# Keys, values and the second half's x turned by VectorE in 32 by 32 blocks and by the transfers

## The chip, the cores and the metric

The kernel runs on one core of a Trainium2 chip. The metric is the device time of one execution in microseconds (us). The engines are named as in the profile: PE (TensorE, with PEld for its weight loads), DVE (VectorE), ACT (ScalarE), POOL (GpSimd) and SP (SyncE, which here only issues transfers).

## The reference, cut to what matters

One decoder layer over a prompt of 2048 tokens of width 1024 (and 32 sample tokens), all in fp32. One wide projection feeds two mixers:

```python
h = rmsnorm(x, g_norm)
proj = jnp.einsum('bld,de->ble', h, w_in)                 # 1024 -> 10240 columns
u_p, z_p, q, k, v, z_r, gates = jnp.split(proj, IN_SPLITS, axis=-1)
...
qh, kh = rope(q, pos), rope(k, pos) * RET_QK_DIM ** -0.5  # 4 heads of 256
scores = jnp.einsum('bhid,bhjd->bhij', q, k) * decay      # inside a chunk
inner  = jnp.einsum('bhij,bhjv->bhiv', scores, v)         # v: 4 heads of 512
s_new  = gamma ** C * s + jnp.einsum('bhjd,bhjv->bhdv', k_dec, v)
...
x_out = x + jnp.einsum('bld,de->ble', merged, w_out)      # then rmsnorm
```

The projection comes out with features on the partitions and tokens along the rows. The state update (`s_new`) contracts over tokens, so it wants keys and values with tokens on the partitions: they have to be turned. So has x, whose rows arrive with tokens on the partitions while the projection contracts over features.

## The kernel before

**Numbers.** Each fp32 matrix is split into a high and a low fp32r part; one product is three multiplications (high by high, low by high, high by low), lines 1310 to 1312.

**First part: the projection.** The prompt is two halves of 1024 tokens, each half 40 jobs (`NJ`): 32 for the heads and 8 for the gates. A job is 256 columns of `w_in` against the 1024 tokens by a seven-product scheme (Strassen's, Winograd's form): seven products of 12 multiplications of 128x512, in the order A11B11, A12B21, S2T2, S1T1, S3T3, S4B22, A22T4. Below, product i of a job is numbered 0 to 6 in this order. A head's eight jobs are q, v, k, v, zp, u, z, z. In the first half the heads come first and then the eight gates; in the second half seven gates, the heads, the last gate.

**Who does what in a job j.** SP loads the weights of job j+2 (1 MB, `weights`), then stores the results of job j-1 (`store`). ACT splits off the high part of the weights, DVE the low part, both six products ahead of PE (`SLOTS`). POOL makes the sums of weights. ACT copies partial sums out of PSUM after products 0, 2 and 3 (`part_s`, `part_v`, `part_s` again) and DVE adds after products 1, 4 and 5 into `c_out`. PE may start product 5 (S4B22) of a job only when the second `part_s` copy is made (`s5_copied`), and ACT makes that copy only when DVE has made its addition of product 1 (`c11_done`). That addition writes `c_out[j % 2]`, and so waits until the stores of job j-2 from the same buffer have landed (`c_free`).

**Turning keys and values.** After job j-1 was a k or v, PE turns its result in four steps after products 1 to 4 of job j (`turn`, four transposes of 128x128 each, L1360); ACT takes the high part from PSUM (`turn_high`), DVE the low part (`turn_low`, L2329) into one of three buffers `turned`, and SP stores 512 KB from it (L767). Keys also go through `rope` on DVE, and their unturned form is stored too, high and low (L774, L775), after `rope_low`.

**The second half's x.** From product 3 of job 32 on, every 11 products (`APART`) one of four pairs of token tiles is worked: SP loads it (`x_rows`), ACT squares (offset 1), DVE and POOL normalise (2 and 3) and make the sums (4), PE transposes the seven operands (offsets 5 to 9, L1305), ACT copies each out of PSUM and issues its store to `x_d` (L1810, L1813). SP may load the next pair when PE has transposed the last. After the fourth pair SP loads the seven operands back (`x_load`, L740) and ACT and DVE split them just before the second half starts.

**Second part: retention, branches, output.** Four token blocks of 512, four heads each. SP loads each head's q, k, turned k, v and z and, behind them in the same queue, the weights of the branches in pieces (`raw`, four buffers); ACT and DVE split them five pieces ahead of PE.

## Time and profile before

| | |
|---|---|
| median of 3 runs (lowest to highest) | 2841.2 us (2833.3 to 3100.54) |
| the profiled execution, its own time | 2833.4 us |
| its span | 2831.6 us |
| PE busy, of the span | 98% |
| DVE, ACT, POOL busy | 64%, 40%, 24% |
| TensorE clock granted | 0.997 |
| DMA queue q1 (SP): packets, MB, share of 16 engines | 266279, 541.73, 53.5% |
| DMA queue q10 (ACT): the same | 15168, 8.46, 1.0% |

Time outside the span is 1.8 us. Busy times of PE count the overlap of one multiplication with the next, so what PE's work costs is read from the distance of the starts in the timeline.

### The profile page before, as it was taken

The page shows a single profiled execution, that of the slowest core. Times are in us where ns is not written, and L with a number is a line of the kernel's source. Part 1 is how long each engine was busy: PE and PEld are TensorE (multiplying, and loading weights), DVE is VectorE, ACT ScalarE, POOL GpSimd, SP SyncE. Part 2 cuts the span into 40 slices and gives each one's busy share as a digit, 9 for nine tenths or more (in the row PEclk, how much of TensorE's full clock was granted, in tenths as well). Part 3 has the DMA queues.
Part 4 walks back from the last instruction along what each step waited for, and adds up shares of the span by engine and source line. Part 5 has one row for each costly group of instructions (what it writes and reads, how often), then busy time and mean ns, then how long its engine had stood idle before and what let it go on. Part 6 is the DMA issues. An engine that isn't in the chain of part 4 may idle for free.

```text
span 2831.6 us, 36714 instructions
## 1 busy us (share of the span) xinstructions
PE 2782.2 (98%) x13504; PEld 2249.1 (79%) x13504; DVE 1808.3 (64%) x2588; ACT 1126.4 (40%) x1901; POOL 684.8 (24%) x456
## 2 busy tenths in 40 slices
PE   6999999999999999999999999999999999999998
PEld 5888888888877777777777787877887888788876
DVE  8667566667555365655755566676677667766775
ACT  5444444444554444443434433333333333333332
POOL 5253433434332223425334330000000000000000
PEclk9999999999999999999999999999999999999999
DMA  4544444454564344453444458487648764876496
GB/s 144 197 146 155 173 147 158 156 179 145 180 223 153 113 156 162 147 186 125 163 154 154 165 200 307 141 278 289 246 145 283 289 239 150 283 290 234 153 340 261
DMA packets 281849, 552.80 MB, mean 195 GB/s; under 512 B 24216, under 2 KB 166872, under 8 KB 270527
## 3 DMA queue, kind: packets, MB, share of 16 engines
q1 hardware_dynamic: 266279, 541.73, 53.5%
q10 hardware_dynamic: 15168, 8.46, 1.0%
q8 instruction: 110, 1.80, 0.3%
q14 instruction: 68, 0.56, 0.1%
q0 software_dynamic: 224, 0.26, 0.0%
HBM read 375.59 MB, written 175.14 MB: 194 GB/s over the span
## 4 chain that ended last, share of the span: by engine, by line
PE 90%; DVE 4%; DMA 2%; issue 2%; ACT 1%; POOL 0%; ACTq 0%; SPq 0%; DVEq 0%; POOLq 0%
PE bank L1310 28%; PE bank L1312 28%; PE bank L1311 28%; PE bank L1360 2%; PE bank L1383 1%; PE bank L1502 1%; DMA raw<-in_w_branch_ret 1%; DVE w_lo L2173 1%; DVE xa_lo L2173 1%; DVE xs L2187 1%; PE bank L1632 1%; PE bank L1620 0%; PE bank L1610 0%; DMA x_d<-x_out 0%; DMA raw<-in_w_branch_pool 0%
## 5 line engine op out<-in xcount | busy, mean ns | idle before, releaser
L1310 PE MATMUL bank<-xa_hi,wa_hi 128*128 128x512 f32 x2240 | 888.8, 397 | 5.5 <-ACT part_s L1864 3.2
L1312 PE MATMUL bank<-xa_hi,wa_lo 128*128 128x512 f32 x2240 | 873.6, 390 | 0.0
L1311 PE MATMUL bank<-xa_lo,wa_hi 128*128 128x512 f32 x2240 | 873.5, 390 | 0.0
L1310 PEld LDWEIGHTS bank<-xa_hi,wa_hi 128*128 128x128 f32 x2240 | 420.6, 188 | 107.8 <-issue 21.5
L1312 PEld LDWEIGHTS bank<-xa_hi,wa_lo 128*128 128x128 f32 x2240 | 420.5, 188 | 90.0
L1311 PEld LDWEIGHTS bank<-xa_lo,wa_hi 128*128 128x128 f32 x2240 | 421.1, 188 | 82.8
L2173 DVE TENSOR_TENSOR wa_lo<-w_raw,wa_hi 128x512 fp32r<-128x512 f32 x320 | 312.7, 978 | 165.9 <-ACT wa_hi L1857 165.1
L2173 DVE TENSOR_TENSOR wa_lo<-w_sum,wa_hi 128x512 fp32r<-128x512 f32 x240 | 194.2, 809 | 241.3 <-ACT wa_hi L1857 241.3
L2173 DVE TENSOR_TENSOR w_lo<-raw,w_hi 128x512 fp32r<-128x512 f32 (+1 forms) x288 | 181.9, 659 | 189.3 <-ACT w_hi L1971 189.2
L1857 ACT ACTIVATE wa_hi<-w_raw 128x512 fp32r<-128x512 f32 x320 | 201.2, 629 | 242.6 <-PE bank L1312 238.3
L1971 ACT ACTIVATE w_hi<-raw 128x512 fp32r<-128x512 f32 (+1 forms) x288 | 166.4, 603 | 306.6 <-PE bank L1312 208.5
L1210 POOL TENSOR_TENSOR w_sum<-w_raw,w_sum 128x512 f32<-128x512 f32 x80 | 127.5, 1594 | 405.1 <-DVE wa_lo L2173 403.2
L1310 PE MATMUL bank<-og_hi,w_hi 128*128 128x512 f32 x512 | 201.4, 393 | 2.0 <-DVE z_in L2456 1.8
L1312 PE MATMUL bank<-og_hi,w_lo 128*128 128x512 f32 x512 | 200.0, 391 | 0.0
L1311 PE MATMUL bank<-z_lo,w_hi 128*128 128x512 f32 x512 | 199.8, 390 | 0.0
L1857 ACT ACTIVATE wa_hi<-w_sum 128x512 fp32r<-128x512 f32 x240 | 150.5, 628 | 105.5 <-PE bank L1312 93.4
L1218 POOL TENSOR_TENSOR w_sum<-w_raw,w_sum 128x512 f32<-128x512 f32 x80 | 113.1, 1414 | 307.8 <-DVE wa_lo L2173 307.8
L1265 POOL TENSOR_TENSOR inv_std<-var_eps,half 128x2 f32<-128x2 f32 x32 | 25.7, 803 | 640.6 <-DVE var_eps L2442 640.6
L1224 POOL TENSOR_TENSOR c_out<-c_out,tmp 128x1024 f32<-128x1024 f32 x48 | 117.8, 2458 | 195.9 <-ACT tmp L1901 195.3
L2173 DVE TENSOR_TENSOR c_out<-bank,part_s 128x512 f32<-128x512 f32 x144 | 98.9, 687 | 84.3 <-PE bank L1312 62.5
L1205 POOL TENSOR_TENSOR w_sum<-w_raw 128x512 f32<-128x512 f32 x80 | 122.8, 1536 | 55.4 <-DVE wa_lo L2173 48.2
L1214 POOL TENSOR_TENSOR w_raw<-w_raw 128x512 f32<-128x512 f32 x80 | 132.7, 1659 | 0.0
(253 smaller groups left out, 4311.8 us busy)
## 6 DMA issues: line engine op xcount, KB each, us to landing
w_raw<-in_w_in SPq DMA_DIRECT2D x80, 1024.0 KB, 5.3
v_d<-turned SPq DMA_DIRECT2D x64, 512.0 KB, 3.2
qk_s<-qk_d SPq DMA_DIRECT2D x32, 1024.0 KB, 7.4
v_s<-v_d SPq DMA_DIRECT2D x32, 1024.0 KB, 11.5
raw<-in_w_branch_ret SPq DMA_DIRECT2D x128, 256.0 KB, 4.2
tabs<-in_c_rope SPq DMA_DIRECT2D x16, 1024.0 KB, 6.9
qk_d<-high SPq DMA_DIRECT2D x32, 512.0 KB, 4.6
qk_d<-c_low SPq DMA_DIRECT2D x32, 512.0 KB, 5.4
```

The lines of the kernel that those rows point to most:

```text
L1205: pool.tensor_tensor(w_sum[:, 0], b12, b11, ALU.subtract).then_inc(w_summed, 1)
L1210: pool.tensor_tensor(w_sum[:, 1], b22, w_sum[:, 0], ALU.subtract).then_inc(w_summed, 1)
L1214: pool.tensor_tensor(b12, b22, b12, ALU.subtract).then_inc(w_summed, 1)
L1218: pool.tensor_tensor(w_sum[:, 1], b21, w_sum[:, 1], ALU.subtract).then_inc(w_summed, 1)
L1224: pool.tensor_tensor(c_out[:, j % 2, t], c_out[:, j % 2, t], tmp[t][:], ALU.mult).then_inc(z_mul, 1)
L1310: pe.matmul(out, lh, rh, start=first, stop=False, skip_group_check=onto)
L1311: pe.matmul(out, lh, rl, start=False, stop=False, skip_group_check=onto)
L1312: return pe.matmul(out, ll, rh, start=False, stop=last, skip_group_check=onto)
L1360: mm = pe.transpose(banks[6 + q % 2][:, (2 * i + e) * P:(2 * i + e + 1) * P], c_out[:, j % 2, t, e, tile * P:(tile + 1) * P], ident[:])
L1857: act.activation(wa_hi[:, n % SLOTS], src, ACT.Copy).then_inc(wa_hi_done, 1)
L1971: act.activation(w_hi[:, u % RING, 0:width], raw[:, u % RAW, 0:width], ACT.Copy).then_inc(w_hi_done, 1)
L2173: return dve.tensor_tensor(out, a, b_, op).then_inc(s, 1)
```

## The change

PE no longer turns keys, values or the second half's x. DVE transposes them in 32 by 32 blocks (`turn_blocks`, `x_turn_blocks`: values and x in place, keys into the table buffer `tabs`), which leaves each block turned but not moved, and the transfers put the blocks where they belong: each store becomes four, one for each 32 partitions, and writes pieces of 256 B (keys), 512 B (values) or 128 B (x) to the scratch tensors, whose layouts change. The columns of v's weights and the rows of the rotated keys and queries are interleaved to fit, so the queries' and keys' own stores become four of 32 partitions as well, two rows of 2 KB for each partition. The high and low parts of what is turned are taken from SBUF instead of PSUM. The x stores move from ACT to SP, without the copy out of PSUM. In the second part the turned keys come in by four loads instead of one, and the final state goes out by sixteen stores instead of four.

```diff
-SPREAD = (0, 1, 1, 2, 3, 3, 4)
+SPREAD = (0, 0, 1, 1, 2, 2, 3)
...
-        kt_d = scratch("kt_d", [NB, HEADS, NC, P, 2, 2, DK])
-        v_d = scratch("v_d", [NB, HEADS, NC, P, 2, 2, DV])
+        kt_d = scratch("kt_d", [NB, HEADS, BT, T // BT, 2, BA, 2 * BT])
+        v_d = scratch("v_d", [NB, HEADS, NT, P, 2, BA, 4 * BT])
...
-        x_d = scratch("x_d", [PROD, P, KH, T])
+        x_d = scratch("x_d", [PROD, KH, P, T])
...
+                if kind(i) == "k":
+                    engine.wait_ge(turn_lo, 4 * before(i + 1, "k", "v"))
...
-            return {"q": 64, "k": 64, "v": 0}.get(kind(j), 32)
+            return {"q": 64 * BA, "k": 64 * BA, "v": 0}.get(kind(j), 32)
...
-                engine.wait_ge(turn_mm, 4 * before(j - 1, "k", "v"))
+                engine.wait_ge(turn_lo, 4 * before(j - 1, "k", "v"))
...
+        def weight_columns(j, rows, e):
+
+            w = w_raw[:, j % 2, rows, :]
+            if kind(j) == "v":
+                return w.rearrange("p k (a e s) -> p k a e s", a=BA, e=2)[:, :, :, e, :]
+            return w[:, :, e * P:(e + 1) * P]
...
+        def turned_source(j, q):
+
+            t, c = q // 2, q % 2
+            if kind(j) == "v":
+                return c_out[:, j % 2, t, :, c * CHUNK:(c + 1) * CHUNK].rearrange("p e (b s) -> p b e s", s=BT)
+            return tabs[:, c, t * T:(t + 1) * T].rearrange("p (b e s) -> p b e s", b=8, e=2)
...
-                engine.wait_ge(t_stored[n % TURNED], 16 * (n // TURNED))
+                engine.wait_ge(t_stored[n % TURNED], 16 * BA * (n // TURNED))
...
+                if n > PAIRS:
+                    x_pair_stored(sp, n - 1)
...
+            def x_store(n, i):
+                x_operand_ready(sp, n, i)
+                for a in range(XA):
+                    t = (n - PAIRS) * P + a * XB
+                    sp.dma_start(x_d[i][:, :, t:t + XB].rearrange("k (b r) t -> r (k b) t", b=XA),
+                                  x_operand(n, i)[a * XB:(a + 1) * XB, :].rearrange("r (b t) -> r b t", t=XB))\
+                        .then_inc(x_stored, 16)
...
+            def rotated(j, t):
+                what, i, _part = JOBS[j]
+                b = 2 * (j // NJ) + t
+                sp.wait_ge(qk_lo_done, 2 * before(j, "q", "k") + t + 1)
+                dst = qk_d[b, i, "qk".index(what)]
+                for low, src in enumerate((qk_high[t], c_low[:, j % 2, t])):
+                    for a in range(BA):
+                        rows = dst[a % 2 * 2 * BT:(a % 2 + 1) * 2 * BT, low, a // 2]
+                        sp.dma_start(rows.rearrange("(e s) t -> s e t", e=2),
+                                     src[a * BT:(a + 1) * BT].bitcast(F32)).then_inc(c_stored[j % 2], 16)
...
-                        dst = kt_d[b, i, c] if what == "k" else v_d[b, i, c][:, :, :, part * DK:(part + 1) * DK]
-                        sp.dma_start(dst, turned[:, n % TURNED].bitcast(F32)).then_inc(t_stored[n % TURNED], 16)
+                        if what == "k" and c:
+                            rotated(j, q // 2)
+                        for a in range(BA):
+                            src = turned[a * BT:(a + 1) * BT, n % TURNED].bitcast(F32)
+                            if what == "v":
+                                dst = v_d[b, i, 2 * c:2 * c + 2, :, part, a].rearrange("n (b r) x -> r (n b) x", b=BA)
+                                sp.dma_start(dst, src.rearrange("r b h e s -> r b (h e s)"))\
+                                    .then_inc(t_stored[n % TURNED], 16)
+                                continue
+                            dst = kt_d[b, i, :, 8 * c:8 * c + 8, :, a, :].rearrange("r b h x -> r (b h) x")
+                            sp.dma_start(dst, src.rearrange("r b h e s -> r (b h) (e s)")).then_inc(t_stored[n % TURNED], 16)
...
-                    if what in ("q", "k"):
-                        sp.wait_ge(qk_lo_done, 2 * before(j, "q", "k") + t + 1)
-                        dst = qk_d[b, i, "qk".index(what)]
-                        sp.dma_start(dst[:, 0], qk_high[t][:].bitcast(F32)).then_inc(c_stored[j % 2], 16)
-                        sp.dma_start(dst[:, 1], c_low[:, j % 2, t].bitcast(F32)).then_inc(c_stored[j % 2], 16)
+                    if what == "q":
+                        rotated(j, t)
...
+            def keys_of_chunk(s, b, h, c):
+                src = kt_d[b, h, :, 8 * c:8 * c + 8].rearrange("r (i b) h a x -> b r i (h a x)", b=BA)
+                for i in range(BA):
+                    dst = kt_s[s][i * BT:(i + 1) * BT, c].bitcast(F32).rearrange("p i h d -> p i (h d)")
+                    sp.dma_start(dst, src[i]).then_inc(tv_arrived[s][c], 16)
...
+                    for k in range(PROD):
+                        n = step(j, i, 5 + SPREAD[k])
+                        if n is not None:
+                            x_store(n, BESIDE[k])
...
-                    sp.dma_start(io["ret_prompt"][0, 0, p].rearrange("(k p) v -> p k v", p=P), state[:, p])\
-                        .then_inc(state_stored, 16)
+                    final = io["ret_prompt"][0, 0, p].rearrange("(e k a s) v -> a e s k v", e=2, k=2, a=2)
+                    for part in range(BA):
+                        sp.dma_start(final[part // 2, part % 2], state[part * BT:(part + 1) * BT, p]).then_inc(state_stored, 16)
...
-                    if j and kind(j - 1) in ("k", "v") and 1 <= i < 5:
-                        turn(j - 1, i - 1)
-                    for k in range(PROD):
-                        n = step(j, i, 5 + SPREAD[k])
-                        if n is not None:
-                            m = PROD * (n - PAIRS) + k
-                            if m < 2:
-                                pe.wait_ge(turn_lo, 4 * before(NJ, "k", "v"))
-                                pe.wait_ge(r_step, r_x_done)
-                            else:
-                                pe.wait_ge(x_copied, m - 1)
-                            x_transposes(n, BESIDE[k], 6 + m % 2)
...
-            def x_copy(n, k):
-                m = PROD * (n - PAIRS) + k
-                act.wait_ge(x_turned, PROD * PAIRS + m + 1)
-                if m >= 4:
-                    act.wait_ge(x_stored[m % 4], 16 * (m // 4))
-                else:
-                    all_turned_stored(act, NJ)
-                    act.wait_ge(r_step, r_turned)
-                    act.wait_ge(r_step, r_squared)
-                act.activation(x_out[:, m % 4, :], banks[6 + m % 2][:], ACT.Copy).then_inc(x_copied, 1)
-                w = slice((n - PAIRS) * P, (n - PAIRS + 1) * P)
-                act.wait_ge(x_copied, m + 1)
-                act.dma_start(x_d[BESIDE[k]][:, :, w], x_out[:, m % 4, :].rearrange("p (k t) -> p k t", k=KH))\
-                    .then_inc(x_stored[m % 4], 16)
 
...
+            def x_turn_blocks(n):
+                buf = x_place(n)[0]
+                dve.wait_ge(x_normed, 2 * n + 2)
+                for t in range(2):
+                    for half in range(2):
+                        own = xs[buf][:, t, half * 512:(half + 1) * 512]
+                        dve.transpose(own, own).then_inc(x_blocks, 1)
...
+            def turn_blocks(j, t):
+                if kind(j) == "k":
+                    dve.wait_ge(rope_done, 2 * before(j, "q", "k") + t + 1)
+                elif t == 0:
+                    dve.wait_ge(c11_done, j + 1)
+                    dve.wait_ge(c12_done, j + 1)
+                else:
+                    dve.wait_ge(c21_done, j + 1)
+                    dve.wait_ge(c22_done, j + 1)
+                for e in range(2):
+                    src = c_out[:, j % 2, t, e, :]
+                    if kind(j) == "k":
+                        src = src.rearrange("p (c b s) -> p c b s", c=2, s=BT)
+                    dve.transpose(blocks(j, t, e), src).then_inc(blocks_turned, 1)
...
+                    if j and kind(j - 1) == "k" and i in (2, 4):
+                        rope_low(j - 1, i // 2 - 1)
...
+                    if j and kind(j - 1) in ("k", "v") and i == 0:
+                        turn_blocks(j - 1, 0)
...
+                    if j and kind(j - 1) in ("k", "v") and i == 1:
+                        turn_blocks(j - 1, 1)
```

What the change moves, at the places that matter. First SyncE's queue in the first half, from the stores of the head's q to the v after its k. Before:

```order
L774 DMA qk_d<-high_79 128x1024
L775 DMA qk_d<-c_low 128x1024
L774 DMA qk_d<-high_80 128x1024
L775 DMA qk_d<-c_low 128x1024
L747 DMA w_raw<-in_w_in 128x8x256
L767 DMA v_d<-turned 512x1x256 x4
L747 DMA w_raw<-in_w_in 128x8x256
L767 DMA kt_d<-turned 128x1024 x4
```

And after the change, from the v's stores on:

```order
L830 DMA v_d<-turned 32x8x128 x16
L794 DMA w_raw<-in_w_in 128x8x256
L834 DMA kt_d<-turned 32x16x64 x4
L813 DMA qk_d<-high_79 32x2x512 x4
L813 DMA qk_d<-c_low 32x2x512 x4
L834 DMA kt_d<-turned 32x16x64 x8
L813 DMA qk_d<-high_80 32x2x512 x4
L813 DMA qk_d<-c_low 32x2x512 x4
L834 DMA kt_d<-turned 32x16x64 x4
L794 DMA w_raw<-in_w_in 128x8x256
```

A key job had 8 stores and has 32; its rotated keys (`high_79` and `high_80` are the high parts of the two token tiles) now stand between its turned ones instead of behind them, and the next weights stand behind all of it.

Second, VectorE in the job behind a k, after the change (`tmp_78` and `tabs` belong to the rotation of the second token tile):

```order
L2194 TENSOR_TENSOR wa_lo<-w_sum,wa_hi 128x512
L2368 STREAM_TRANSPOSE tabs<-c_out 128x2x8x32 x2
L2194 TENSOR_TENSOR tmp_78<-c_out,tabs 128x1024
L2194 TENSOR_TENSOR c_out<-c_out,tabs 128x1024
L2194 TENSOR_TENSOR c_out<-bank,part_s 128x512
L2194 TENSOR_TENSOR wa_lo<-w_raw,wa_hi 128x512
L2194 TENSOR_TENSOR c_out<-c_out,tmp_78 128x512 x2
L2368 STREAM_TRANSPOSE tabs<-c_out 128x2x8x32 x2
L2194 TENSOR_TENSOR c_low<-c_out,high_79 128x1024
L2377 SCALAR_TENSOR_TENSOR turned<-tabs,turned 128x8x64
```

Four transposes of blocks and the first `c_low` now stand ahead of the first `turned`, which is what the first store of turned keys waits for; before, only the rotation stood ahead of it.

Third, SyncE's queue at the first pair of x of the second half, after the change:

```order
L759 DMA xs_82<-in_x_prompt 128x2x1024
L794 DMA w_raw<-in_w_in 128x8x256
L852 DMA gate_d<-c_out 128x1024 x2
L765 DMA x_d<-xs_82 32x16x32 x12
L765 DMA x_d<-xq_86 32x16x32 x16
L759 DMA xs_82<-in_x_prompt 128x2x1024
```

Between the loads of two pairs SP now issues 28 stores of x; before, it issued none, and ACT seven.

## Rows read from the trace of the kernel before

**Rows 1.** The page's engines (busy, share, instructions) and its chain by engine.
```profile
PE 2782.2 (98%) x13504; PEld 2249.1 (79%) x13504; DVE 1808.3 (64%) x2588; ACT 1126.4 (40%) x1901; POOL 684.8 (24%) x456
...
PE 90%; DVE 4%; DMA 2%; issue 2%; ACT 1%; POOL 0%; ACTq 0%; SPq 0%; DVEq 0%; POOLq 0%
```

**Rows 2.** Timeline of TensorE (start, duration us), one product alone: first multiplication to the next.
```profile
60.12 0.39 PE L1310 MATMUL bank<-xa_hi,wa_hi 128*128 128x512 f32 x1
...
62.84 0.39 PE L1310 MATMUL bank<-xa_hi,wa_hi 128*128 128x512 f32 x1
```

**Rows 3.** Timeline of TensorE, the same with one turn between products.
```profile
86.99 0.48 PE L1310 MATMUL bank<-xa_hi,wa_hi 128*128 128x512 f32 x1
...
89.83 0.60 PE L1360 MATMUL bank<-ident,c_out 128*128 128x128 f32 x4
...
90.19 0.48 PE L1310 MATMUL bank<-xa_hi,wa_hi 128*128 128x512 f32 x1
```

**Rows 4.** Groups by line; and from the timeline one x turn.
```profile
L1360 PE MATMUL bank<-ident,c_out 128*128 128x128 f32 x384 | 57.6, 272 | 0.0
...
709.08 0.60 PE L1305 MATMUL bank<-ident,xq 128*128 128x128 f32 x4
```

**Rows 5.** Groups by line and form on VectorE (count, busy us, mean ns).
```profile
L2329 DVE SCALAR_TENSOR_TENSOR turned<-bank,turned 128x512 fp32r<-128x512 f32 x96 | 65.8, 686 | 65.0 <-ACT turned L1907 65.0
...
L2173 DVE TENSOR_TENSOR wa_lo<-w_raw,wa_hi 128x512 fp32r<-128x512 f32 x320 | 312.7, 978 | 165.9 <-ACT wa_hi L1857 165.1
```

**Rows 6.** Timeline of VectorE in the first key head's turning.
```profile
113.20 0.68 DVE L2329 SCALAR_TENSOR_TENSOR turned<-bank,turned 128x512 fp32r<-128x512 f32 x1
...
116.66 1.22 DVE L2173 TENSOR_TENSOR c_low<-c_out,high 128x1024 fp32r<-128x1024 f32 x1
...
131.20 0.69 DVE L2173 TENSOR_TENSOR c_out<-bank,part_s 128x512 f32<-128x512 f32 x1 [3.29 <-DMA qk_d<-c_low]
```

**Rows 7.** Timeline of ScalarE there: first and fourth copies of the products' partial sums.
```profile
105.05 0.60 ACT L1864 ACTIVATE part_s<-bank 128x512 f32<-128x512 f32 x1 [1.60 <-PE bank L1312]
...
126.07 0.60 ACT L1864 ACTIVATE part_s<-bank 128x512 f32<-128x512 f32 x1 [1.60 <-PE bank L1312]
...
135.18 0.60 ACT L1873 ACTIVATE part_s<-bank 128x512 f32<-128x512 f32 x1 [1.59 <-PE bank L1312]
...
138.37 0.64 ACT L1857 ACTIVATE wa_hi<-w_sum 128x512 fp32r<-128x512 f32 x1 [1.10 <-PE bank L1312]
```

**Rows 8.** Timeline of SyncE's queue: the last stores of that key job.
```profile
122.31 0.43 SPq L774 DMA_DIRECT2D qk_d<-high  x1
...
124.86 1.20 SPq L775 DMA_DIRECT2D qk_d<-c_low  x1
```

**Rows 9.** DMA queues in three windows: 690 to 735, 20 to 30, 91.5 to 103 us.
```profile
q10 hardware_dynamic: 3696, 1.84, 13.9%
...
q1 hardware_dynamic: 2120, 0.07, 13.3%
...
q1 hardware_dynamic: 1883, 1.88, 48.1%
```

**Rows 10.** DMA rows: the x stores' issue (ns min/median/max); issues of x loads.
```profile
L1813 ACTq DMA_DIRECT2D x_d<-x_out x28: 520/521/594, 703.6 to 822.7; - x28
...
xs<-in_x_prompt SPq DMA_DIRECT2D x8, 1024.0 KB, 6.9
```

**Rows 11.** Timelines of VectorE, SyncE and ScalarE around one pair of x.
```profile
702.49 0.68 DVE L2173 TENSOR_TENSOR xq<-xs 128x512 f32<-128x512 f32 x1
...
716.53 0.38 SPq L718 DMA_DIRECT2D xs<-in_x_prompt  x1
...
725.28 1.04 ACT L1793 ACTIVATE xq<-xs 128x1024 f32<-128x1024 f32 x1
...
727.47 0.60 ACT L1869 ACTIVATE part_v<-bank 128x512 f32<-128x512 f32 x1
```

**Rows 12.** Chain of waits in the last token block.
```profile
2707.00 8.80 DMA raw<-in_w_branch_pool
```

165 lines of the change are left out of this document (77 added, 88 removed).

## The prediction

> **What bounds the kernel now.** I read first the page's line of engines and the chain by engine: PE is busy for 98% of the span and holds 90% of the chain [rows 1]. So time goes when work leaves PE, as long as nothing else then makes PE wait. Busy times of PE overlap, so the second view is its timeline, for distances of starts. A product alone takes 62.84 - 60.12 = 2.72 us [rows 2]; with one turn of four transposes behind it, 90.19 - 86.99 = 3.20 us [rows 3]. A turn costs 0.48 us, and a job without turns 7 x 2.72 = 19.05 us. The third view is the timelines of DVE, ACT and SP around a key's turning, for the waits that are covered today and how much cover they have; the fourth the same around a pair of x; the fifth the DMA queues in short windows, for the price of a small piece.
>
> **What leaves PE.** The group has 384 transposes of k and v, 96 turns of four [rows 4]: 96 x 0.48 = 46.1 us. The second half's x has 4 pairs x 7 operands, each again four transposes of the same 0.60 us form [rows 4]: 28 x 0.48 = 13.4 us. Together **59.5 us**, all on the path.
>
> **What a small piece costs.** In 690 to 735 us ACT's queue moved 3696 packets, the x stores' 512 B, in 13.9% of 16 engines: 0.139 x 16 x 45 / 3696 = 27 ns each. Loads of 4 B took 0.133 x 16 x 10 / 2120 = 10 ns, stores of 1 KB 0.481 x 16 x 11.5 / 1883 = 47 ns [rows 9]. Stores of 256 B and 128 B don't occur. Between 10 and 27 ns a line through both gives 18.5 and 14 ns; I take these, since the 1 KB store lies close to the same line, and keep 10 and 27 as ends.
>
> The Trainium skill (DMA: Bandwidth & Descriptors, Specifications) says that below 512 B a transfer no longer runs at line rate, since the engine reads, modifies and writes. No row here shows it; by it the line is wrong on the cheap side, which is the third rival below.
>
> **The key job, term by term.** Let T be the end of product 0 of the job behind k, 105.05 [rows 7]. Today the first low part of the keys starts at T + 8.15 [rows 6]. Ahead of it now also stand four transposes of 128x512 on DVE and the first `c_low` of 1.22 us [rows 6]. A block transpose is not in the trace; the nearest row is a 128x512 operation at 686 ns, and one that shares time with POOL takes 978 [rows 5]. I take 0.69 (ends 0.35 and 1.0). So the first low part ends at T + 8.15 + 4 x 0.69 + 1.22 + 0.69 = T + 12.8. DVE itself holds: four transposes are 2.8 us in a job, with six products of lead, and I count 2 us in all for it.
>
> SP then issues 4 stores of keys, 8 of rotated keys, 8 of keys, 8 of rotated keys. An issue with 512 pieces takes 0.52 us [rows 10], one of the rotated kind 0.43 [rows 8]: 12 x 0.52 + 16 x 0.43 = 13.1, so the last rotated store is issued at T + 26. The engines need, for three quarters of the keys, 3 x 2048 x 18.5 / 16 = 7.1 us, and for 2 MB of rotated keys 6.2 us at the rate of the 1 KB stores (1.88 MB in 0.481 x 11.5 us, 340 GB/s [rows 9]) or up to twice that, since every engine now reads from the same 32 partitions: done at T + 26 to 32. To complete I add 2 us: today 8.9 us pass from 122.31 to the landing before 131.20 [rows 6, 8], of which the 2 MB take 6.2, so 2.7 is the most. The last rotated store lands at T + 28 to 34.
>
> Who waits for it: DVE's addition after product 1 of the job two behind k, which writes the same `c_out`. It waits already today, 3.29 us, until 131.20, T + 26.2 [rows 6]. This delays nothing, since ACT's copy that needs it comes at 135.18 and PE's product 5 starts at 138.37 [rows 7]. After the change the jobs are shorter: product 4 of that job ends at T + 19.05 + 4 x 2.72 = T + 29.9, and for an ACT copy of 0.60 and a DVE addition of 0.69 before it the stores must land by T + 28.6. The cover, today 5 us, is gone. I take 30, in the lower half, since rows of 2 KB are large pieces: 1.5 us in each of 8 key jobs, **12 us**. Ends: 0 (landing at 28), and at 27 ns a piece 3.3 us more on top of the slow rotated stores, 8.7 x 8 = 70 us.
>
> Edits at nothing: v's 16 stores a job (4096 pieces x 27 / 16 = 6.9 us in a 19 us job, beside 1 MB of weights); the interleaved columns on ACT, DVE and POOL, same sizes and rows of 128 B; the next weights behind the stores, issued about T + 28 and needed by ACT at T + 41.
>
> **x.** Today DVE begins the sums at 702.49, SP issues the next pair's load at 716.53 and ACT begins its squares at 725.28 [rows 11]. Now four transposes (2.8 us) come before the sums, then 28 stores from SP, 28 x 0.52 = 14.6 us, while the engines need 14336 x 14 / 16 = 12.5 us: SP's issue sets the pace. The load leaves at 702.5 + 2.8 + 14.6 + 2.5 for the last to land = 722.4 and brings x, in the median 6.9 us later [rows 10], at 729.3. PE without seven turns would have the squares at 725.28 - 3.3 = 722. ACT's next copy, at 727.47 right behind the squares [rows 11], has about 2 us before PE's next but one product wants it. Stall 5 us for each of the three pairs loaded so; minus 1 each, since the median load had other transfers beside it: **12 us**. Ends: 0, and at 27 ns a piece (24.2 us instead of 14.6) 3 x 14 = 42 us. The seven loads back after the fourth pair had more cover; 0 there, and 5 at the upper end.
>
> **Second part.** Keys come in by 32-partition loads, 4 instead of 1 for each chunk, ahead of the branch weights in the queue; the final states go out by 16 stores just where the last block's chain already holds 8.80 us of waiting for `raw` [rows 12]. If these move at half rate, some 5 us more there or in the heads before: **5 us** (0 to 15). The values as PE's moving operand come in runs of 256 B instead of whole rows; no row shows such an operand beside a dense one, I take 0 and put 5% of 672 multiplications, 672 x 0.227 x 0.05 = 8 us, at the upper end.
>
> **Sum.** -59.5 + 12 + 12 + 5 + 2 = -28.5 us against the profiled execution's 2833.4: **2805 us**. That execution lies 0.3% under the median of 2841.2, so the forecast is 1.3% under the median.
>
> **Rivals.**
>
> *All covers hold.* If the stores land at T + 28 and the x loads are back in time, the time is 2833 - 59 + 2 = 2776 to 2784. For: PE waits for almost nothing today. Against: both waits' cover is used up within a microsecond by my own count. 0.13.
>
> *The queue becomes the bound, but pieces stay at 27 ns or less.* Slow rotated stores and 27 ns: 2833 - 59.5 + 70 + 42 + 15 = 2900; around the middle 2850. For: SP has 28 + 4 issues in a stretch where it had 4 or 8. The Trainium skill (SBUF — State Buffer, Door 1: The DMA port swizzle) has 32 partitions reach only half of the ports, which is this rival's slow rotated store. 0.22.
>
> *Small stores cost like large ones, slower than before.* If a store of 256 or 128 B costs what one of 1 KB does, 47 ns [rows 9]: keys 3 x 2048 x 47 / 16 = 18 us, landing at T + 39 to 45, 10 to 16 us beyond the limit, x 8 = 80 to 130, 93 more than counted in the middle; x 42 us instead of 14.6, 3 x 27.5 more, 82, and about 25 for the last pair: 2805 + 93 + 107 = about 3005. Each nanosecond of piece price costs 3 x 2048 / 16 x 8 = 3.1 us at the keys and 896 x 4 = 3.6 us at x, so it decides from about 30 ns on: there the time passes 2898. 0.18.
>
> *It does not do what it says.* If PE kept transposes of k, v or the second half's x, each turn would keep its 0.48 us; the new order of PE has none of them, so this gets nothing.
>
> The forecast's own case, both waits there but small (2785 to 2830), has 0.47. The range takes in the clean case and nearly all of the queue case: 2775 to 2890. The rest is the third rival. Two per cent is about what a measurement of this kernel can tell from no change: faster by over 2% (under 2784) 0.14, within it 0.68, slower 0.18.
>
> **What would show it.** In the new profile: product to product 2.72 us everywhere; DVE transposes near 0.69 us; the wait of DVE's addition for `qk_d` up from 3 us to 6 or more in each key job, and PE idle behind `part_s` in these 8 places, 1 to 2 us each; ACT's squares waiting for `xs` and about 5 us of PE idle three times near 700 to 800 us; packets under 2 KB at 14 to 20 ns. It would be wrong if small packets took over 30 ns, if a DVE transpose took over 1 us (2.4 us later landing in each key job), or if PE ran slower on the interleaved values.

## The result and the profile after

| | before | after |
|---|---|---|
| median (lowest to highest), us | 2841.5 (2833.3 to 3100.5) | 2869.8 (2867.5 to 2871.3) |
| the profiled execution: its time, its span, us | 2833.4, 2831.6 | 2871.3, 2869.5 |
| granted clock | 0.997 | 0.987 |

The change makes the kernel slower by 1.2%: the ratio is 1.0119, 95% interval 1.0106 to 1.0131. Disturbed runs of the kernel before are left out of it, so it is larger than that of the medians. The forecast was 2805 us, 28 below the kernel before; it came out 38 above. The time lies within the range of 2775 to 2890, but the sign is the other one.

The page of the changed kernel, its engines, its chain and SP's queue, against [rows 1]:

```profile
PE 2753.4 (96%) x13008; PEld 2211.4 (77%) x13008; DVE 1906.0 (66%) x2700; ACT 1112.0 (39%) x1873; POOL 673.1 (23%) x456
...
q1 hardware_dynamic: 448103, 549.11, 60.7%
...
PE 74%; DVE 8%; SPq 6%; DMA 5%; issue 4%; ACT 1%; POOL 1%; DVEq 0%; ACTq 0%; POOLq 0%
```

PE has 496 fewer instructions, the transposes. Its share of the chain falls from 90 to 74%, and SP's queue, DMA and "issue", 4% together before, hold 15%; DVE's share doubles to 8%. PE did lose work; it now waits more than it lost.

**Where.** The start of ACT's first `part_s` copy marks each job in both kernels. Its distance between kernel and kernel before, after job 33 (the first half's heads), job 41 (the x pairs), job 79 (the second half's heads) and at the end of the span, in us:

| kernel | job 33 | job 41 | job 79 | end |
|---|---|---|---|---|
| changed | -4.6 | +13.8 | +2.6 | +37.9 |
| x on TensorE | -6.6 | -6.9 | -17.3 | +13.5 |
| values only | -14.8 | -15.3 | -30.5 | -27.6 |
| one key load a chunk | -5.0 | +13.8 | +2.5 | +7.8 |
| the same, four state stores | -6.7 | +11.1 | +2.0 | +4.0 |
| four key loads, contiguous | -3.3 | +13.9 | +2.3 | +41.2 |
| four key loads, all partitions | -4.0 | +13.1 | +3.5 | +9.9 |
| x in 7 stores, 128 B | -6.3 | +3.5 | -6.4 | +24.1 |
| x in 7 stores, 512 B | -4.3 | -5.3 | -15.8 | +16.2 |
| x on TensorE, rotated whole | -15.0 | -15.1 | -32.6 | -5.0 |
| x on TensorE, keys whole | -8.4 | -8.4 | -21.6 | +7.6 |
| x on TensorE, both whole | -15.4 | -15.3 | -32.8 | -0.9 |
| x on TensorE, small key blocks | -10.9 | -10.9 | -28.7 | -1.3 |
| x on TensorE, rotated ahead, two loads | -6.8 | -5.2 | -19.3 | +90.6 |

So the changed kernel's 38 us are: heads -15.9 (-4.6, and from +13.8 to +2.6), x +18.4, second part +35.3.

How exact such distances are: in five of these executions (four key loads of both kinds, x in 7 stores of 512 B, both whole, small key blocks) the second job already starts 2.0 to 2.3 us later than in the kernel before, in the others 0.2 to 0.6 us. And the eight kernels that share the changed second part lose from 27.4 to 35.3 us in it. So a difference of 2 us in the heads, or of 4 us in the second part, says nothing by itself.

**The key job.** DVE's transposes (groups by line and form), and the first key head's turning in DVE's and SP's timelines; against [rows 5, 6, 8]:

```profile
L2368 DVE STREAM_TRANSPOSE c_out<-c_out 128x512 f32<-128x512 f32 x64 | 41.5, 685 | 0.0
...
L2368 DVE STREAM_TRANSPOSE tabs<-c_out 128x512 f32<-128x512 f32 x32 | 20.8, 689 | 0.3
```
```profile
114.82 0.68 DVE L2377 SCALAR_TENSOR_TENSOR turned<-tabs,turned 128x512 fp32r<-128x512 f32 x1
...
134.88 0.69 DVE L2194 TENSOR_TENSOR c_out<-bank,part_s 128x512 f32<-128x512 f32 x1 [8.03 <-DMA qk_d<-c_low]
```
```profile
115.53 2.21 SPq L834 DMA_DIRECT2D kt_d<-turned  x4
...
123.08 5.13 SPq L834 DMA_DIRECT2D kt_d<-turned  x8
128.32 2.23 SPq L813 DMA_DIRECT2D qk_d<-high  x4
130.60 2.08 SPq L813 DMA_DIRECT2D qk_d<-c_low  x4
```

A transpose takes what was assumed, 0.69 us. T is 103.34 here, so the first low part of the keys ends at T + 12.2 and the last rotated store's wait at T + 31.5; over the eight key jobs it is T + 30.5 to 31.7, where T + 30 was taken. The wait for `qk_d` is 5.9 to 8.2 us instead of 1.9 to 3.6.

What PE waits for in the job two behind k, first in PE's timeline, then the addition in DVE's:

```profile
136.41 0.47 PE L1389 MATMUL bank<-xa_hi,wa_hi 128*128 128x512 f32 x1 [1.77 <-ACT part_s L1899]
140.51 0.47 PE L1389 MATMUL bank<-xa_hi,wa_hi 128*128 128x512 f32 x1 [1.10 <-DVE c_out L2194]
```
```profile
139.69 0.68 DVE L2194 TENSOR_TENSOR c_out<-bank,part_s 128x512 f32<-128x512 f32 x1
```

PE is held twice: at product 5 by the late landing itself (through ACT's copy), and at product 6 by DVE's addition, which comes late because DVE, after its wait for `qk_d`, has transposes, low parts and `turned` to catch up on. The second stall, 1.0 to 1.1 us, is there in seven of the eight key jobs. The first is 0.7 to 1.9 us in the first half and at most 0.2 us in the second half: a job without stalls lasts 20.31 us there, not 19.04, since the sample tokens ride on it, and the landing is in time.

**x.** SP's and ACT's timelines at the second pair, then TensorE in windows (window, length, PE busy and instructions, granted clock, DMA share, GB/s); against [rows 11]:

```profile
735.58 6.33 SPq L765 DMA_DIRECT2D x_d<-xs  x12
741.96 2.14 SPq L765 DMA_DIRECT2D x_d<-xq  x4
745.83 12.58 SPq L765 DMA_DIRECT2D x_d<-xq  x12
759.88 0.40 SPq L759 DMA_DIRECT2D xs<-in_x_prompt  x1
```
```profile
765.45 1.06 ACT L1834 ACTIVATE xq<-xs 128x1024 f32<-128x1024 f32 x1 [10.53 <-DMA xs<-in_x_prompt]
...
769.25 0.58 ACT L1890 ACTIVATE part_s<-bank 128x512 f32<-128x512 f32 x1
```
```profile
762.00:764.00 2.00, 0.00 (x0) 1.00 0.89 356
764.00:766.00 2.00, 0.00 (x0) 0.98 0.06 25
766.00:768.00 2.00, 0.00 (x0) 0.50 0.00 0
768.00:770.00 2.00, 0.03 (x1) 0.50 0.00 0
770.00:772.00 2.00, 2.00 (x5) 0.50 0.02 4
772.00:774.00 2.00, 2.00 (x9) 0.81 0.52 135
774.00:776.00 2.00, 2.00 (x11) 1.00 0.89 265
```

This pair's 28 stores take 22.8 us, not 14.6. ACT stands before the squares for 10.5 us, and behind them, in ACT's program, stand the copies that PE waits for: PE is idle for 8 us. And then PE starts slowly: the granted clock is 0.50, 1.2 instead of 2.4 GHz, and two microseconds hold 5 multiplications instead of 10 or 11.

The seven operands' way back, which the forecast took as covered, costs as well. SP's first loads of them, before and after; ACT's wait for the first, and PE's stalls:

```profile
825.38 1.27 SPq L740 DMA_DIRECT2D x_new<-x_d  x3
```
```profile
839.20 1.48 SPq L787 DMA_DIRECT2D x_new<-x_d  x3
```
```profile
844.91 1.91 ACT L1863 ACTIVATE xa_hi<-x_new 128x2048 fp32r<-128x2048 f32 x1 [6.75 <-DMA x_new<-x_d]
```
```profile
847.45 0.47 PE L1389 MATMUL bank<-xa_hi,wa_hi 128*128 128x512 f32 x1 [4.51 <-ACT part_v L1895]
...
868.29 0.73 PE L1389 MATMUL bank<-xa_hi,wa_hi 128*128 128x512 f32 x1 [3.69 <-ACT part_s L1890]
```

Before, they left 6.2 us ahead of the start of job 39; now they leave 4.4 us behind it, since the fourth pair's 28 stores end at 837.7, and they land 7.5 us after their issue in the median, 4.9 before. ACT waits 13.8 us for them instead of 3.5. Of the x stage's loss over the kernel before, +7.9 us stand at the start of job 39 and 10.5 more come up to job 41.

**Second part.** Its first loads in windows (columns as above), and some of the longest pieces of DMA that the chain holds:

```profile
1681.00:1683.00 2.00, 2.00 (x10) 1.00 1.00 418
1683.00:1685.00 2.00, 2.00 (x10) 1.00 0.99 270
1685.00:1687.00 2.00, 2.00 (x12) 1.00 1.08 224
1687.00:1689.00 2.00, 2.00 (x20) 1.00 1.02 263
1689.00:1691.00 2.00, 0.30 (x3) 0.99 1.02 391
1691.00:1693.00 2.00, 0.45 (x1) 0.50 1.03 412
1693.00:1695.00 2.00, 2.00 (x6) 0.50 1.03 426
```
```profile
1682.29 10.12 DMA v_s<-v_d
...
1730.00 14.66 DMA raw<-in_w_branch_ret
...
1951.94 14.05 DMA raw<-in_w_branch_ret
...
2528.02 13.72 DMA raw<-in_w_branch_ret
```

The DMA share is full all the time, but between 1683 and 1689, while the keys come in by loads of 32 partitions, it moves 224 to 270 GB/s and not 391 to 426. The values land late, PE idles, and the granted clock falls to 0.50 meanwhile. The branch weights `raw` queue behind the same loads; the long pieces stand where a token block begins, and once inside the first block. The kernel before had two such pieces on its chain, of 11.2 and 11.0 us.

### The profile page after: what moved, and what is told of

Its sections match the earlier page's. It is cut to its first block, busy times and chain, and to the rows that moved or that the text cites. A ratio compares the mean times of both kernels' runs of the same rounds, so it can differ in the third digit from the quotient of the medians.

```text
span 2869.5 us, 36374 instructions
## 1 busy us (share of the span) xinstructions
PE 2753.4 (96%) x13008; PEld 2211.4 (77%) x13008; DVE 1906.0 (66%) x2700; ACT 1112.0 (39%) x1873; POOL 673.1 (23%) x456
## 4 chain that ended last, share of the span: by engine, by line
PE 74%; DVE 8%; SPq 6%; DMA 5%; issue 4%; ACT 1%; POOL 1%; DVEq 0%; ACTq 0%; POOLq 0%
PE bank L1389 24%; PE bank L1390 23%; PE bank L1391 23%; SPq L813 2%; SPq L834 2%; DMA raw<-in_w_branch_ret 2%; SPq L765 1%; PE bank L1437 1%; PE bank L1544 1%; DVE c_out L2194 1%; DVE wa_lo L2194 1%; DMA qk_d<-c_low 1%; PE bank L1673 1%; DVE xs L2208 1%; DMA xs<-in_x_prompt 1%
## 5 line engine op out<-in xcount | busy, mean ns | idle before, releaser
L1389 PE MATMUL bank<-xa_hi,wa_hi 128*128 128x512 f32 x2240 | 885.1, 395 | 49.5 <-DVE c_out L2194 18.7
L2194 DVE TENSOR_TENSOR wa_lo<-w_sum,wa_hi 128x512 fp32r<-128x512 f32 x240 | 206.7, 861 | 213.1 <-ACT wa_hi L1883 212.8
L1289 POOL TENSOR_TENSOR w_sum<-w_raw,w_sum 128x512 f32<-128x512 f32 x80 | 122.5, 1532 | 361.5 <-DVE wa_lo L2194 359.6
L1297 POOL TENSOR_TENSOR w_sum<-w_raw,w_sum 128x512 f32<-128x512 f32 x80 | 105.5, 1318 | 347.3 <-DVE wa_lo L2194 347.3
## 6 DMA issues: line engine op xcount, KB each, us to landing
v_s<-v_d SPq DMA_DIRECT2D x32, 1024.0 KB, 12.4
```

Source lines behind the costliest of these rows:

```text
L1289: pool.tensor_tensor(sums[1], b22, sums[0], ALU.subtract).then_inc(w_summed, 1)
L1297: pool.tensor_tensor(sums[1], b21, sums[1], ALU.subtract).then_inc(w_summed, 1)
L1389: pe.matmul(out, lh, rh, start=first, stop=False, skip_group_check=onto)
L2194: return dve.tensor_tensor(out, a, b_, op).then_inc(s, 1)
```

## The experiments

Each was compared with the kernel before on its own chip, whose median there was 2835 to 2837 us; ratios are to that.

**x back on TensorE.** The edit undoes the x part of the diff and keeps keys and values:

```diff
-                    for offset, work in ((2, x_variance), (3, x_normalize), (4, x_turn_blocks), (4, x_sums)):
+                    for offset, work in ((2, x_variance), (3, x_normalize), (4, x_sums)):
```

> The changed kernel with the second half's x turned by TensorE, copied by ACT and stored from ACT's queue again, as before the change; keys and values stay on VectorE. Theory X (the x stage lost more than PE won there: 28 stores issued by SP between a pair's normalization and the next pair's load): the span from the first job of the x stage to the end of it, +18.4 us after against before, goes back to about 0, and the total is 2870 - 18 = 2852 (2847 to 2857). Rival (the x stage lost because of the late keys and values around it, and not by x itself): 28 turns come back on PE, 13.4 us, and nothing else changes: 2883. The second part keeps its +35 us by both.

Measured 2846.8 us, ratio 1.0042 (1.0026 to 1.0058). From job 33 to 41 it changes by -0.3 us instead of +18.4: theory X. Turning x without PE saves 13.4 us and costs 31.8. The total lies at the lower edge of what was expected, since this execution's second part lost 30.8 us and not 35.3.

**The key loads of the second part.** One transfer instead of four:

```diff
-                for i in range(BA):
-                    dst = kt_s[s][i * BT:(i + 1) * BT, c].bitcast(F32).rearrange("p i h d -> p i (h d)")
-                    sp.dma_start(dst, src[i]).then_inc(tv_arrived[s][c], 16)
+                sp.dma_start(kt_s[s][:, c].bitcast(F32).rearrange("p i h d -> p i (h d)"), src)\
+                    .then_inc(tv_arrived[s][c], 16)
```

> The changed kernel, but the second part loads the keys of a chunk by one transfer over 128 partitions, of the same bytes in another order (the output is not the reference's, the keys come in a wrong order), instead of four over 32 partitions. Theory L (the loads hold SP's queue, and the branch weights `raw` behind them come late): most of the second part's +35 us goes away, total 2870 - 20 to 30 = 2840 to 2850, and `raw` waits of 12 to 14 us leave the chain. Rival V (the values as an operand in runs of 256 B, or their stage in memory, slow the second part): total stays within 4 us of 2870. Rival S (only the 16 stores of the final states cost, at the end): within 5 us of 2870 too, with the offset unchanged until the last block.

> As the kernel with one load a chunk, and the final states go out by 4 stores over 128 partitions as before the change (rows in a wrong order, so the output is not the reference's). Theory L expects 2 to 6 us less than with one load alone, since the last block's end lost 4 us after the changed kernel's stores: about 2840. Rival S expects the main part of the 35 us here and not there: about 2840 here against 2866 there.

Measured 2841.2 us, ratio 1.0022 (1.0012 to 1.0032), and 2840.1 us, 1.0018 (1.0008 to 1.0028), with four state stores. From job 79 to the end the first loses 5.3 us, the changed kernel 35.3; the ratios (1.0022 against 1.0119) make it 27.5 us. So the loads cost some 25 to 30 us. The kernel with four state stores loses 2.0 us there, but 3.3 us less is within the scatter and the two ratios don't differ: that the 16 state stores cost anything is not shown. PE multiplies with the values in the same interleaved layout in both, so rival V is out. Rival S is out too.

**Count of loads, DRAM layout or 32 partitions.** Four loads again, from contiguous rows: once 32 partitions each, once all 128 with a quarter of each row:

```diff
+                    rows = slice(i * BT, (i + 1) * BT)
+                    dst = kt_s[s][rows, c].bitcast(F32).rearrange("p i h d -> p i (h d)")
+                    sp.dma_start(dst, src[rows]).then_inc(tv_arrived[s][c], 16)
```
```diff
+                    sp.dma_start(dst[:, i], src[:, i]).then_inc(tv_arrived[s][c], 16)
```

> The changed kernel with four key loads a chunk over 32 partitions each, as in the changed kernel, but each reads one contiguous stretch of DRAM (the bytes of the kernel with one load a chunk, 2841.2 us; keys in a wrong order, so the output is not the reference's). Theory H (a load into 32 partitions runs at half the rate): as slow as the changed kernel, 2864 to 2872. Theory D (rows 32 KB apart in DRAM are what is slow): 2840 to 2848. Theory C (the count of issues): as slow as the changed kernel, too; the next kernel tells C from H.

> The changed kernel with four key loads a chunk, each over all 128 partitions in pieces of 1 KB, from contiguous rows (the keys in a wrong order, so the output is not the reference's). Theory H: near the kernel with one load a chunk, 2841 to 2850. Theory C (four issues instead of one ahead of the branch weights): 2860 to 2872.

Measured 2870.8 us, ratio 1.0120 (1.0098 to 1.0142), and 2845.4 us, 1.0031 (1.0019 to 1.0042). Both have four issues and contiguous rows; only the loads into 32 partitions are slow. The windows of the same stretch, 32 partitions first, then 128:

```profile
1683.00:1685.00 2.00, 2.00 (x10) 1.00 1.04 266
1685.00:1687.00 2.00, 2.00 (x12) 1.00 1.03 225
1687.00:1689.00 2.00, 2.00 (x20) 1.00 1.02 262
```
```profile
1683.00:1685.00 2.00, 2.00 (x10) 1.00 0.88 324
1685.00:1687.00 2.00, 2.00 (x10) 1.00 1.07 363
1687.00:1689.00 2.00, 2.00 (x18) 1.00 1.07 402
```

**Values only.** The kernel before with `turn_blocks`, the weights' interleaved columns, the stores by 32 partitions and the new `v_d` for values alone:

```diff
-                    if j and kind(j - 1) in ("k", "v") and 1 <= i < 5:
+                    if j and kind(j - 1) == "k" and 1 <= i < 5:
                         turn(j - 1, i - 1)
```

> The kernel before, with only the values turned by VectorE in 32 by 32 blocks and stored by 32 partitions; keys, the second half's x, the rotated keys' stores, the key loads and the final states as before. 64 turns leave PE, 64 x 0.48 = 31 us. Theory of covers (a job with values has 6 products of lead and only 16 stores of 256 B pieces, nothing waits for it) and theory L for the second part: 2833 - 31 = 2803 to 2812, faster than both kernels. Rival V (values cost the second part its 35 us): 2833 - 31 + 35 = about 2838. Rival Q (the 16 small stores of the second value job, not the rotated keys, are what made job times uneven, +1.5 to 4 us behind them): 16 jobs x 2 = 32 us lost, about 2835 too, but lost in the first part.

Measured **2807.0 us, ratio 0.9901 (0.9886 to 0.9917)**: the version that beats both kernels. By job 79 it has gained 30.5 us of the 64 x 0.48 = 30.7. Its second part loses 2.9.

**The key job's stores.** On the kernel with x on TensorE, the rotated stores over 128 partitions (first line), or those of the turned keys (second), or both:

```diff
+                    sp.dma_start(dst[:, low], src.bitcast(F32)).then_inc(c_stored[j % 2], 16)
...
+                            sp.dma_start(dst, turned[:, n % TURNED].bitcast(F32).rearrange("p b h e s -> p (b h) (e s)"))\
+                                .then_inc(t_stored[n % TURNED], 16)
```

> On the kernel with x back on TensorE (2846.8 us, job 79 at -17.3 us against before, where the 96 turns alone would give -46.1): the rotated keys and queries go out by 4 stores a job over 128 partitions, as before the change, instead of 16 over 32 (rows in another order, so the output is not the reference's). Theory I (the count of issues sets when `c_out` comes free: 28 issues of about 0.6 us lie ahead of the last rotated store's end): 12 issues fewer, 7 us earlier, the wait of 46.5 us in 7 places for `qk_d` and the idle time of PE behind `c_out` go; job 79 at -38 to -46, total 2818 to 2826. Theory P (the 256 B pieces of the turned keys fill the engines and hold the queue): the last store lands less than 2 us earlier, job 79 at -17 to -22, total 2842 to 2847. Theory H (stores from 32 partitions run at half the rate): as theory I.

> On the same kernel, x on TensorE: the turned keys go out by 4 stores a job over 128 partitions instead of 16 over 32, in the same number of pieces of 256 B (their places are other ones, so the output is not the reference's); the rotated keys keep their 16 stores over 32 partitions. Theory I: of the 28 issues ahead 9 are gone, 5 us earlier, job 79 at -34 to -46, total 2818 to 2830. Theory P: pieces are as many, job 79 at -17 to -22. Theory H: the rotated stores stay slow; job 79 between -17 and -30.

> The kernel with x on TensorE and both the rotated keys' stores and the turned keys' stores over 128 partitions, 4 + 4 ... each as in the two kernels that change one of them (job 79 at -32.6 and -21.6 us; -17.3 with neither; the output is not the reference's). If the two gains add: -32.6 - 4.3 = -37. If together they free the wait for `c_out` and what is left is the second value job alone, as with the values alone: -46. If the 256 B pieces themselves are what is left: no better than -37. Total 2822 to 2829, the second part still with its 30 us.

Measured 2831.9 (ratio 0.9985, 0.9975 to 0.9995), 2840.5 (1.0016, 1.0007 to 1.0026) and 2830.3 us (0.9982, 0.9972 to 0.9991). `c_out` comes free at T + 28.3 to 29.2 with the rotated stores whole, and at T + 27.0 to 28.6 with both, against T + 30.1 to 31.3. By job 79 the rotated stores bring 15.3 us, those of the keys 4.3, both 15.5, or 17 without this execution's 2 us at the start: they don't add. With both, the job two behind k has no stall left in seven of the eight places; what is missing to -46 is DVE's 11.5 us (below) and those 2. With the rotated stores whole, PE still loses 0.4 to 0.7 us in each of the first half's four jobs, though the stores land 1.2 to 1.6 us before its limit there (worked out below): the landing alone doesn't set the loss. Both forecasts of theory I for a total (2818 to 2826, and to 2830) are missed. Theory I fails by its count: nine issues fewer bring 4.3 us, twelve bring 15.3. The slow rotated stores, theory H, fit better, but their count changed with their width, so the two are not separated here. What the total then lacks is the second part's 30 us, which all three keep.

**The rotated stores ahead, and two key loads.**

```diff
-                        if what == "k" and c:
+                        if what == "k" and not c:
                             rotated(j, q // 2)
...
+                src = kt_d[b, h, :, 8 * c:8 * c + 8].rearrange("r (i b) h a x -> i b r (h a x)", b=BA)
```

> On the same kernel, x on TensorE, two changes that keep the result: the rotated keys of each half are issued ahead of the half's first turned keys instead of ahead of its second (the last rotated store is then issue 24 and not 28), and the second part loads a chunk's keys by 2 transfers over 128 partitions instead of 4 over 32. First part, theory I: 4 issues, 2.3 us earlier in each key job, 8 x 2.3 = 18 us, job 79 at -30 to -36; theory P: less than 1 us earlier, job 79 at -17 to -22, or later than before if the turned keys now hold `turned`. Second part, theory L (time per load): half of the loads gone beyond one gives two thirds of the 30 us, 20 us; if it is the 32 partitions and not the count that costs, nearly all of the 30. Total 2809 to 2830.

Measured 2928.2 us, ratio 1.0326 (1.0310 to 1.0342). The order brings 2 us by job 79, not 18: the job behind the key job, 20.48 us in the first half of the other kernels with full transposes of keys, becomes 22.7 to 23.1 us long, and the jobs behind it win back little more than that. The two loads lose 110 us from job 79 to the end, which no theory had. Windows of SP's queue (granted clock, DMA share, GB/s) behind two pairs of these loads:

```profile
1720.00:1722.00 2.00, 1.00 0.33 114
1722.00:1724.00 2.00, 1.00 0.27 101
1724.00:1726.00 2.00, 1.00 0.26 100
```

A share of 0.26 is four of the 16 engines. The source of these loads has an outermost dimension of 4 where the others have 32 or 128. That the loads are dealt out to the engines by it is a reading of the share; it wasn't tried apart.

**Fewer x stores.** On the changed kernel, 7 stores a pair over all partitions, in pieces of 128 B, and then of 512 B:

```diff
+                sp.dma_start(dst[:, :, t:t + XB], x_operand(n, i).rearrange("p (m t) -> p m t", t=XB))\
...
+                sp.dma_start(x_d[i][:, :, t:t + P].rearrange("k p t -> p k t"),
+                             x_operand(n, i).rearrange("p (k t) -> p k t", t=P)).then_inc(x_stored, 16)
```

> The changed kernel with the second half's x stored by 7 transfers a pair over 128 partitions instead of 28 over 32, in as many pieces of 128 B (other places, so the output is not the reference's). Theory I (SP's issue, 0.52 us for each of 28 stores, holds the next pair's load): 21 issues fewer are 11 us earlier for each of the three loads, and PE's idle time there goes; the x stage gives back 20 to 30 us, total 2840 to 2850. Theory P (14336 pieces of 128 B set the pace): the stores last as long, total within 5 us of 2870, and the 7 issues are held back. A middle result gives the price of a piece.

> The changed kernel with the second half's x stored by 7 transfers a pair over 128 partitions in pieces of 512 B, a quarter of the pieces of the kernel with 7 transfers of 128 B (2857.2 us, x stage +9.9 us) (order of the elements inside is another, so the output is not the reference's). If the time that the pieces take holds the next pair's load (theory P for x): 3584 pieces of 27 ns on 16 engines are 6 us a pair instead of 12.5, the stage gives back another 3 x 6 = 18 us or until nothing waits, total 2838 to 2846. If what is left is that the load may only start when the last operand is summed and stored, whatever the pieces (theory W): within 5 us of 2857.

Measured 2857.2 us, ratio 1.0077 (1.0062 to 1.0092), and 2849.0 us, 1.0048 (1.0033 to 1.0063). From job 33 to 41 the offset changes by +18.4 us with 28 stores, by +9.8 with 7 stores of 128 B, and by -1.0 with 7 of 512 B. So both count, 8.6 us for the issues and the width, 10.8 for the pieces; theory P alone and W are out, I gave less than it asked, and the last total is 3 us above theory P's range. The rest, 12.4 us above the 13.4 that the turns save, lies in two places: 6.9 us up to job 39, where ACT still waits 4.7 us for the second pair and PE 3.6 us for DVE, and 5.5 us at the seven loads back. They leave as early against job 39 as before (their last four 9.7 us behind its start, 9.5 before), but land after 7.8 us in the median, not 4.9, and ACT waits 7.7 us for them. Whether that is the new layout of `x_d` or the traffic beside them isn't separated. SP's queue during such stores, pieces of 128 B in 5 us and of 512 B in 3 us:

```profile
q1 hardware_dynamic: 5673, 0.72, 91.2%
```
```profile
q1 hardware_dynamic: 1728, 0.86, 102.6%
```

That is 0.912 x 16 x 5 / 5673 = 12.9 ns and 1.026 x 16 x 3 / 1728 = 28.5 ns a piece; 14 and 27 were taken.

**DVE's transposes in the key job.** The job right behind the key job lasts 20.48 us and not 19.04 in the first half, and 21.7 and not 20.31 in the second, in each kernel that has the keys on DVE but the one with the rotated stores ahead. Here DVE transposes 128x32 each time instead of 128x512:

```diff
+                    if kind(j) == "k":
+                        dve.transpose(blocks(j, t, e)[:, 0, 0, :], src[:, 0, 0, :]).then_inc(blocks_turned, 1)
+                        continue
```

> The kernel with x on TensorE, where DVE's four transposes of 128x512 in each key job are 128x32 instead (they turn a corner of the block; the turned keys are not the reference's), with all waits and transfers as they were. In every kernel with keys on DVE the job behind the key job lasts 20.48 us, not 19.04, whatever its stores; with the values alone on DVE that job has PE's turns and lasts 21.02. Theory B (DVE is the one that is late in that job: 4 x 0.6 us of transposes between the weights' low parts): it lasts 19.04 us, 8 x 1.44 = 11.5 us less by the end of the first part, and as the low parts of the keys start 2.4 us earlier, the stores end earlier and up to 2.4 us of each late landing goes as well; job 79 at -29 to -46, total 2818 to 2836. Rival (ACT's or SP's share in that job, the same without the transposes): 20.48 us stays, total 2847.

Measured 2834.6 us, ratio 0.9997 (0.9987 to 1.0006). That job lasts 19.03 to 19.04 us in the first half and 20.30 to 20.31 in the second: the 11.5 us of theory B, 8 x 1.44, are shown by the jobs themselves. Job 79 is at -28.7, 11.3 us less than with full transposes, or 13 without the 2 us at this execution's start, the lower edge of what was expected: of the late landing at most 2 us went as well. What PE waited for there, in the changed kernel (waits from 60 to 700 us: total, times, longest):

```profile
PEld bank L1389 <- DVE wa_lo L2194: 16.2, 11, 2.3
...
PE bank L1389 <- DVE c_out L2194: 6.8, 7, 1.1
...
PE bank L1389 <- ACT part_s L1899: 5.0, 4, 1.9
```

The list gives the idle time of the weight loads to DVE's low parts and PE's own to DVE's additions. In the timeline of the first key head the addition ends last: the low part at 117.31, the addition at 117.91, PE starts at 118.06. Four of the seven waits for `c_out` are this one, 0.9 us each; three are the one at product 6 a job later.

## Why the prediction was wrong

Its sum against the runs, in us:

| term | forecast | measured |
|---|---|---|
| turns that leave PE | -59.5 | -59.5 |
| DVE's own time in the key job | +2 | +11.5 |
| the key job's late landing | +12 | +18.7 |
| x pairs | +12 | +21.3 |
| x, the seven loads back | 0 | +10.5 |
| second part | +5 | +35.3 |
| sum | -28.5 | +37.8 |

The first row is not measured by itself; values only gained 1.91 us in each of 16 jobs. The second is 8 x (20.48 - 19.04), the third what is left of the heads' 46.1 - 15.9 = 30.2. The fourth is 7.9 + 13.4 up to job 39, the fifth what comes from there to job 41; together they are the 31.8.

**Second part: the step that failed.** "If these move at half rate, some 5 us more there" had the right mechanism, and its size was a guess: +5 us where the runs showed +35.3, some 25 to 30 of them by the 32 partitions of the key loads. The rate was not even half: about 0.7 of that over 128 partitions in the same three windows (266, 225, 262 against 324, 363, 402 GB/s). Multiplied out, the sentence would have given more: 32 chunks of 512 KB at half of the 340 GB/s that the prediction has are 1.5 us more each, 49 us of a queue that `raw` stands in; at the measured 224 against 400 GB/s 1.0 us each, 33 us. Its upper end of 15 was as arbitrary. This term alone turns the forecast's sign: 30 us more than the -28.5. The doubt was put on the values as an operand in runs of 256 B, which cost nothing: one load a chunk takes those 25 to 30 us away and leaves that operand.

**x.** The price of a piece was right, 12.9 ns for 14, and so was the first pair: its load left at 717.91, in a kernel that was 4.6 us ahead, so 722.5 by the clock of the forecast's 722.4, and PE stood 4.0 us. What failed is "stall 5 us for each": one pair stands for all three. PE stands 8.2 us at the second pair, 3.9 more behind DVE's addition after that pair's normalisation, transposes and sums, and 1.5 us at the third. The second pair's last 12 stores start late, at 745.83, behind the next weights and a gate's two stores, and take 1.05 us each instead of 0.52, so its load leaves 24.3 us after the first store. "The seven loads back after the fourth pair had more cover; 0 there" failed too: 10.5 us, past its upper end of 5, for no row was read for that cover, and the 28 stores stand ahead of these loads like ahead of the others. And PE's loss isn't the idle time alone. Between 690 and 900 us its waits in the list are 26.0 us against 4.0 before; the windows from 700 to 900 have a granted clock of 0.93, 0.90, 0.98 and 0.95, which is 12 us at most (four times 50 us by what is missing to 1.00). Together that is 34 us at most, for the 31.8.

**Late landing.** The stores landed at T + 30.5 to 31.7 for T + 30, and PE lost 2.3 us a key job, not 1.5. That this is near is in part luck. The limit of T + 28.6 was reckoned with a job of 19.05 us; with the 20.48 that DVE makes of it, it is T + 30.1, and with the second half's 21.7, by the same reckoning, T + 32.0. So the landing is 0.4 to 1.6 us late in the first half and 0.8 to 1.4 us early in the second, where PE still loses 1.3 to 1.9 us a key job: through DVE's backlog behind its wait, which the prediction doesn't have, at product 6.

**DVE.** "Six products of lead" was taken as cover for 2.8 us of transposes. In the job behind the key job that lead is already used by `rope`, and the addition that frees product 6's PSUM bank stands behind the transposes in DVE's order; of 2.8 us PE paid 1.44.

**Rivals.** The queue rival (2850 to 2900) had the total, 2871, but not its parts: at its upper end it put 70 us in the key job, 42 at x and 15 in the second part, where 30.2, 31.8 and 35.3 were lost. It rests on the Trainium skill's rule (SBUF — State Buffer, Door 1: The DMA port swizzle) that 32 partitions reach half the ports. For loads the runs go the same way, if not by half: 225 to 266 GB/s against 324 to 402 for the same bytes over 128 partitions. It was weighed at 0.22 and priced only for the stores; there the rotated stores' width and count were not separated. Small stores at the price of large ones did not happen: the rule of the Trainium skill (DMA: Bandwidth & Descriptors, Specifications) that below 512 B an engine reads, modifies and writes would have made 128 B pieces dearer than the line, and they were on it.

## What to carry to other kernels

A layout that moves work from an engine to the transfers is paid wherever the layout is read and written, so multiply out every later load of it too, at the rate of its partitions, with what stands behind it in the queue. Move only the part whose stores nobody waits for: here the values, two thirds of the turning, gave all that was counted for them. For a repeated stage count each repetition's collisions, not the first one's, and the way back too; and add the slower clock behind each idle stretch. Reckon a limit with the job lengths of the kernel after: an engine that is late moves it, and what it has to catch up on behind a wait is a stall of its own.

## What the runs showed of the hardware

- Loads into 32 partitions, with the loads beside them, moved 224 to 270 GB/s at a full DMA share, whether their rows were contiguous or 32 KB apart; in the same windows, with four loads over 128 partitions, it was 324 to 402.
- After PE had been idle, the granted clock was 0.50 (1.2 GHz) until some microseconds after work came back: 0.50 at 770 to 772 us and 0.81 in the next two, and 0.50 from 1691 to 1695. A stall cost more than its idle time.
- Loads with an outermost source dimension of 4 left the DMA share at 0.26 to 0.33 and 100 to 114 GB/s, and with them the second part lost 110 us, where the same bytes by 32 partitions lost 27 to 39.
- Pieces of 128 B took 12.9 ns and of 512 B 28.5 ns, near the line through 4 B at 10 ns.
- A matrix multiplication whose moving operand lies in runs of 256 B took no longer: 389 ns in the median, as before.
- A 32 by 32 block transpose of 128x512 fp32 on VectorE took 685 to 689 ns, as long as a 128x512 subtraction there.
